# Three more places for expert weights, rows in chunk order and another order in the mix stage of a two-layer encoder step

## What is computed

```python
for i in range(2):
    proj = x @ w_in                       # split into attention, HGRN2 and gate columns
    a = latent_attention(...); o = hgrn2(...)
    merged = sigmoid(ga) * (a @ w_br_a) + sigmoid(gb) * (o @ w_br_b)
    x = layernorm(ALPHA * x + merged @ w_out, ln1_g, ln1_b)
    g_prob = softmax(x @ w_rg); e = softmax(x @ w_re within the top group); top 2 of 8
    moe = sum over the 2 experts of wts * ((silu(x @ w1[e]) * (x @ w3[e])) @ w2[e])   # 32 experts
    ple = sigmoid(x @ w_ple_gate) * (p[i] @ w_ple)
    x = layernorm(ALPHA * x + moe + ple, ln2_g, ln2_b)
```

## Time and profile before

| | us |
|---|---|
| median of 3 runs | 1827.39 |
| lowest, highest | 1825.66, 1830.17 |
| the profiled execution | 1829.14 |
| its span, first to last instruction | 1827.4 |

### The profile page before, as it was taken

How to read it: one execution, slowest core, us unless ns; L and a number is a source line. 1 busy time by engine, 2 the same in 40 slices (tenths; PEclk the granted TensorE clock), 3 DMA queues, 4 the chain that set the end, 5 groups by cost and what they waited for, 6 DMA issues and landing times.

```text
span 1827.4 us, 21052 instructions
## 1 busy us (share of the span) xinstructions
PE 1469.8 (80%) x8984; PEld 736.4 (40%) x8985; DVE 470.6 (26%) x1009; ACT 266.9 (15%) x649; POOL 49.7 (3%) x95
## 2 busy tenths in 40 slices
PE   5999879999977767766697998799999777577752
PEld 3556554554432223321253655545544332133310
DVE  3231661162110111100313417513512110111003
ACT  2332321111100000000134323111111000000001
POOL 1200000000000000000021000000000000000000
PEclk9999898998998889878798998799989997888886
DMA  8302213474999999999741032046469999999991
GB/s 296 114 1 93 98 52 128 170 291 167 426 426 426 426 427 426 426 427 426 288 166 48 2 134 102 11 164 244 176 250 426 426 426 427 426 426 427 426 427 79
DMA packets 97458, 491.04 MB, mean 269 GB/s; under 512 B 9264, under 2 KB 15184, under 8 KB 47696
## 3 DMA queue, kind: packets, MB, share of 16 engines
q1 hardware_dynamic: 92608, 478.16, 64.3%
q0 software_dynamic: 4752, 11.45, 1.9%
HBM read 486.69 MB, written 2.89 MB: 268 GB/s over the span
## 4 chain that ended last, share of the span: by engine, by line
PE 53%; DMA 22%; SPq 13%; DVE 5%; issue 3%; ACT 2%; DVEq 0%; POOL 0%; ACTq 0%
PE bank L785 50%; DMA ring<-in_w_e_up 14%; SPq L645 13%; DMA ring<-in_w_e_down 5%; DMA arena<-in_w_e_up 3%; PE bank L812 3%; DVE arena L1819 1%; DMA lnw<-in_ln_b 1%; DVE arena L1820 1%; DVE arena L1852 1%; PE bank L1217 0%; DVE arena L1644 0%; DVE x_sb L1644 0%; DVE x_sb L1649 0%; DVE x_sb L1651 0%
## 5 line engine op out<-in xcount | busy, mean ns | idle before, releaser
L785 PE MATMUL bank<-arena 128*32 128x512 f32 (+12 forms) x2392 | 596.4, 529 | 253.8 <-DMA ring<-in_w_e_up 82.3
L785 PE MATMUL bank<-ring,arena 128*32 128x512 f32 (+4 forms) x1976 | 489.8, 629 | 26.1 <-DMA arena<-in_w_e_gate 12.4
L785 PE MATMUL bank<-ring,xT 128*32 128x128 f32 (+5 forms) x2496 | 451.9, 398 | 7.9 <-issue 4.0
L785 PEld LDWEIGHTS bank<-arena 128*32 128x32 f32 (+7 forms) x2392 | 226.5, 154 | 574.3 <-issue 557.9
L785 PEld LDWEIGHTS bank<-ring,xT 128*32 128x32 f32 (+1 forms) x2496 | 221.9, 144 | 218.5 <-issue 198.9
L785 PEld LDWEIGHTS bank<-ring,arena 128*32 128x32 f32 (+1 forms) x1976 | 135.7, 132 | 122.6 <-issue 115.5
L785 PE MATMUL bank<-arena,x_sb 128*128 128x128 f32 (+1 forms) x768 | 146.0, 323 | 2.5 <-DVE arena L1982 1.9
L785 PE MATMUL bank<-cst,arena 128*32 128x512 f32 (+2 forms) x256 | 135.8, 672 | 0.1
L785 PEld LDWEIGHTS bank<-arena,x_sb 128*128 128x128 f32 (+1 forms) x768 | 111.5, 200 | 45.3 <-issue 16.9
L785 PE MATMUL bank<-lb,arena 128*32 128x512 f32 x160 | 88.4, 705 | 0.0
L2050 DVE TENSOR_TENSOR arena<-arena,bank 128x512 f32<-128x512 f32 x16 | 11.0, 688 | 275.1 <-PE bank L785 275.1
(11 more groups left out here) (218 smaller groups left out, 862.4 us busy)
## 6 DMA issues: line engine op xcount, KB each, us to landing
ring<-in_w_e_up SPq DMA_DIRECT2D x66, 1024.0 KB, 26.6
ring<-in_w_e_down SPq DMA_DIRECT2D x60, 1024.0 KB, 26.7
arena<-in_w_e_gate SPq DMA_DIRECT2D x58, 1024.0 KB, 25.7
ring<-in_w_e_gate SPq DMA_DIRECT2D x50, 1024.0 KB, 26.9
arena<-in_w_e_down SPq DMA_DIRECT2D x48, 1024.0 KB, 26.3
arena<-in_w_e_up SPq DMA_DIRECT2D x44, 1024.0 KB, 26.3
ring<-in_w_in SPq DMA_DIRECT2D x32, 1024.0 KB, 9.1
cst<-in_w_e_gate SPq DMA_DIRECT2D x10, 1024.0 KB, 26.5
```

Source lines behind the costliest of these rows:

```text
L785: return pe.matmul(out, lhsT, rhs, start=first, stop=last, skip_group_check=True)
```

## The change

- Slots: 9 arena slots in place of 7, and the place of the norm rows (LNW_SLOT) once per layer, for one piece of U of quad 0: 21 in place of 18. The working area before the slots shrinks by 768 words, since the input p (pin) now lies where the gathered tokens come later; the arena grows by 3328 words per partition, and the DMA scratch area shrinks to 4096 bytes.
- The host lays out x, the rows of LN0 and LN1 and those of LN2 of layer 0 in chunk order. x is loaded in place. In layer 0 the sums are kept in chunk order too (`by_chunks`), so that the banks are read with a stride of 8 when they are added; in layer 1, whose result is stored, all stays in the natural order.
- POOL loads LN2's rows after U of quad 0.
- Mix stage: the output product of tile 1's second half is cut in two (`project_half`) with the router of tile 0 between; the low product of tile 0 comes before the transposes of tile 1; the gate product of tile 0 is cut in two, around the ranks. DVE routes tile 0 before the last residual add.

```diff
-ARENA_SLOTS = 7
-LEVEL_SLOT, LB_SLOT, XT_SLOT = RING + ARENA_SLOTS, RING + ARENA_SLOTS + 1, RING + ARENA_SLOTS + 2
-SLOTS = RING + ARENA_SLOTS + 3
+ARENA_SLOTS = 9
+LEVEL_SLOT, LB_SLOT, XT_SLOT, LNW_SLOT = range(RING + ARENA_SLOTS, RING + ARENA_SLOTS + 4)
+SLOTS = RING + ARENA_SLOTS + 4
...
+def chunk_order(a):
+    return np.ascontiguousarray(a.reshape(a.shape[:-1] + (P, 8)).swapaxes(-1, -2).reshape(a.shape))
...
-            (("wo", 0, 1), 6), (("rt", 2), 7), (("t1", 0, 0), 0), (("t1", 0, 1), 1), (("wo", 1, 1), 2), (("rt", 0), 3),
-            (("pl", 0, 2), 4), (("pg", 0, 2), 5), (("t1", 1, 0), 6), (("t1", 1, 1), 7), (("pl", 0, 0), 0), (("rt", 1), 1),
-            (("pg", 0, 0), 2), (("rk", 0), 3), (("rk", 1), 6), (("rk", 2), 7), (("cnt",), 1),
+            (("wo", 0, 1), 6), (("rt", 2), 7), (("t1", 0, 0), 0), (("t1", 0, 1), 1), (("rt", 0), 3), (("wo", 1, 1), 2),
+            (("pl", 0, 2), 4), (("pg", 0, 2), 5), (("pl", 0, 0), 0), (("t1", 1, 0), 6), (("t1", 1, 1), 7), (("rt", 1), 1),
+            (("rk", 0), 3), (("rk", 1), 6), (("rk", 2), 7), (("cnt",), 1), (("pg", 0, 0), 2),
...
-    turns += [(2, i) for i in wo]
+    turns += [(2, i) for i in wo] + [(2.5, LNW_SLOT)]
...
-        turns.append((half, i))
+        if i != LNW_SLOT:
+            turns.append((half, i))
...
-        ARENA, FIRST_SLOT = 23520, 9184
+        FIRST_SLOT = 8416
+        ARENA = FIRST_SLOT + ARENA_SLOTS * SLOT
...
-        def sums(t, j):
-            return acc[:, t, 512 * j:512 * j + 512] if t < 2 else acc2[:, P * j:P * j + P]
+        def by_chunks(layer):
+            return layer < DEPTH - 1
+        def sums(layer, t, j):
+            if t == 2:
+                return acc2[:, P * j:P * j + P]
+            if by_chunks(layer):
+                return acc[:, t, :].rearrange("q (c p) -> q c p", c=8)[:, :, 64 * j:64 * j + 64]
+            return acc[:, t, 512 * j:512 * j + 512]
+        def for_sums(layer, t, b):
+            return by_chunk(b[:, :]) if t < 2 and by_chunks(layer) else b[:, 0:held(t)]
...
+                    elif i == LNW_SLOT:
+                        sp.wait_ge(ln_out, 3 * (2 * layer + 1) + 3)
...
-                sp.dma_start(x_given[0:NT[t], t, :], src).then_inc(x_in, 16)
+                sp.dma_start(x[0:NT[t], t, :], src).then_inc(x_in, 16)
...
                 load_ln(1 + 2 * layer, ln1_g[layer], ln1_b[layer])
+                job_done(pool, (layer, "moe", 0, "U"))
                 load_ln(2 + 2 * layer, ln2_g[layer], ln2_b[layer])
...
+            def project_half(layer, key, t, lhs, names, h):
+                n = piece_number(layer, names[h])
+                arrived(n)
+                b = open_bank((layer,) + key + (t,)) if h == 0 else bank((layer,) + key + (t,))
+                w = slot(n).rearrange("p (c n) -> p c n", c=4)
+                for c in range(4):
+                    ins = mm(b[0:NT[t], :], lhs[:, 4 * h + c, T0[t]:T0[t] + NT[t]], w[:, c, :], h + c == 0, h + c == 4)
+                if h == 1:
+                    done(ins)
...
                 turn_mixed(0)
-                mix(1, 1)
+                half_mix = lambda h: project_half(layer, ("wo", 1), 1, mT, [("wo", 1, 0), ("wo", 1, 1)], h)
+                half_mix(0)
                 router(0)
+                half_mix(1)
                 for t in range(3):
                     job_read(pe, (layer, "pT", t))
                 plain(0, 2)
+                plain_low(0, 0)
                 turn_mixed(1)
-                plain_low(0, 0)
                 router(1)
-                plain_high(0, 0)
+                half_gate = lambda h: project_half(layer, ("pg", 0), 0, xT, [("pg", 0, 0), ("pg", 0, 1)], h)
+                half_gate(0)
...
                 done(ins)
+                half_gate(1)
...
-                if k % 2:
-                    a, gain = x_chunks(t), by_chunk(gain)
-                else:
-                    a = src[0:n, :]
-                step(dve.scalar_tensor_tensor(a, a, mean, gain, ALU.subtract, ALU.mult))
+                step(dve.scalar_tensor_tensor(src[0:n, :], src[0:n, :], mvs[0:n, 2 * t:2 * t + 1], lnw[0:n, 0, :],
+                                              ALU.subtract, ALU.mult))
...
                 route_tile(2)
+                route_tile(0)
                 mixed(1, 1)
                 norm_mixed(1)
                 read_x("t1", layer, xT, (1,))
-                route_tile(0)
                 route_tile(1)
...
-                        emptied(dve.tensor_tensor(a, a, bank(key)[:, 0:a.shape[1]], ALU.add), key)
+                        emptied(dve.tensor_tensor(a, a, src, ALU.add), key)
...
-    nc = bacc.Bacc("TRN2", target_bir_lowering=False, num_devices=1)
+    nc = bacc.Bacc("TRN2", target_bir_lowering=False, num_devices=1, dynamic_dma_scratch_size=4096)
...
+    for n in ("x_prompt", "x_sample", "ln0_g", "ln0_b", "ln1_g", "ln1_b"):
+        arrays[f"in_{n}"] = chunk_order(arrays[f"in_{n}"])
+    for n in ("ln2_g", "ln2_b"):
+        rows = arrays[f"in_{n}"]
+        arrays[f"in_{n}"] = np.concatenate([chunk_order(rows[:-1]), rows[-1:]])
```

More of the change, by code:

```diff
@@ L303 @@
 SLOT_OF, FILLS, BEFORE = place_pieces()
+LNW_PIECES = [divmod(SLOT_OF[layer * LAYER_PIECES:].index(LNW_SLOT) - len(PIECES), len(MOE_PIECES)) for layer in range(DEPTH)]
+assert all(g == 0 and MOE_PIECES[i][0] == "eu" for g, i in LNW_PIECES)
 LEVELS_GONE = max(n for n in range(LAYER_PIECES) if SLOT_OF[n] == LEVEL_SLOT)
@@ L1551, in plain_gate @@
                     job_done(act, key)
-                    emptied(act.activation(sums(t, j), bank(key)[:, 0:held(t)], ACT.Sigmoid), key)
+                    emptied(act.activation(sums(layer, t, j), for_sums(layer, t, bank(key)), ACT.Sigmoid), key)
                 for t in MIX_ORDER:
@@ L2018, in gated @@
                 def gated(j, t):
-                    a, w = sums(t, j), held(t)
+                    a, w = sums(layer, t, j), held(t)
                     key = (layer, "pl", j, t)
@@ L2023, in gated @@
                     job_read(dve, (layer, "pg", j, t))
[L2024 removed]
+                    emptied(dve.tensor_tensor(a, a, for_sums(layer, t, bank(key)), ALU.mult), key)
                     if t < 2:
                         job_read(dve, key)
[L2027 removed]
+                        a = a if by_chunks(layer) else by_chunk(a)
+                        step(dve.scalar_tensor_tensor(a, x_chunks(t, w * j, w), ALPHA, a, ALU.mult, ALU.add))
                 def read_tokens(key):
@@ L2098, in more @@
                         for j in range(2):
-                            a = acc[:, t, 512 * j:512 * j + 512]
-                            dve.tensor_tensor(a, a, banks[2 * t + j][:, :], ALU.add)
+                            a = sums(layer, t, j)
+                            dve.tensor_tensor(a, a, for_sums(layer, t, banks[2 * t + j]), ALU.add)
                     a = acc2
@@ L2110, in _ @@
                 xt = acc_s[0:DEC, :]
-                step(dve.scalar_tensor_tensor(by_chunk(xt), x_chunks(2), ALPHA, by_chunk(xt), ALU.mult, ALU.add))
+                if by_chunks(layer):
+                    step(dve.scalar_tensor_tensor(xt, x[0:DEC, 2, :], ALPHA, xt, ALU.mult, ALU.add))
+                else:
+                    step(dve.scalar_tensor_tensor(by_chunk(xt), x_chunks(2), ALPHA, by_chunk(xt), ALU.mult, ALU.add))
                 layer_norm(2 + 2 * layer, 2, acc_s)
```

62 lines of the change are left out of this document (30 added, 32 removed).

## The result

| | before | changed kernel |
|---|---|---|
| median | 1827.54 us | 1800.80 us |
| lowest, highest | 1825.66, 1830.17 (4 runs) | 1799.12, 1801.73 (4 runs) |
| the profiled execution | 1829.14 us | 1801.73 us |
| its span | 1827.4 us | 1799.9 us |

The ratio is 0.985, with a 95% interval of 0.9835 to 0.9864: 26.7 us less. The forecast was 1801. That it came so near was partly luck: the two large terms, the streams and the gather, came as forecast, but four others were off (the norm at the start, the norm at the end of layer 0, the order of the mix stage, the scratch area), and their errors cancelled. The views of the changed kernel show which.

The account below looks back on a forecast made before the run. DMA was taken to bound each layer's expert stream, PE and its waits the rest. Slots 9.0, norms 1.6, mix order 2.2 and gather clock 14.6 sum to 27.4 us less: 1801 us, range 1797 to 1806.

Parts of the forecast that it names:

- Slots: Expert streams: three more pieces placed before each stream save 7.4 us, LN2's rows cost 2.9; net 4.5 per layer, 9.0 in all.
- the third slot: Piece at the norm rows' place, before each stream: saves 2.5 us, but LN2's rows then cost 2.9, so about nothing.
- The clock in the gather: First gather before quad 0: dense half product ahead keeps full clock, 8.5 us; gain 7.3 per layer, 14.6 in all.
- Rivals 1 and 2: Clock still falls in the first gather: in one layer, 1808 us, chance 0.14; in both, 1816 us, chance 0.09.
- Order of the mix stage: Output product of tile 1 to gather: reordering takes 25.9 us, gaining 3.2 and 1.6; net 2.2 after a clock allowance.
- The term for the fall: Mix stage: waits of about 0.9 and 0.8 us around the transposes may lower the clock; 1.3 us per layer, between 0 and 3.
- Norms at the start: Tile 0 of LN0: contiguous scale-and-shift takes 1.285 us instead of 2.07, 0.79 less on the path.
- Norm at the end of layer 0: Tile 0 of LN2: contiguous scale-and-shift is 0.79 us shorter on the path; 1.6 together with the start.
- Sums in chunk order: Layer 0 adds reading the bank at a stride of 8 cost nothing: 0.69 us against 0.689 contiguous.
- Scratch: DMA scratch of a quarter: costs between 0 and 1 us, taken as 0, judged by POOL's mask loads.
- Rivals 3 and 4: PE frees slots too late, streams get gaps: 1810 us, chance 0.04; or the stream's rate falls: 1842 at 405 GB/s, 0.04.

Follow-up runs that it names:

- no_lnw: Changed kernel with 9 arena slots but no piece at the place of the norm rows, and LN2's rows loaded early again: 1798.96 us.
- gate_split_only: Kernel before with one edit, the gate product of tile 0 cut in two around the ranks: 1813.71 us, ratio 0.9928.
- gate_whole: Changed kernel with the gate product of tile 0 in one piece before the ranks: 1811.01 us.
- order_undone: Changed kernel with the old order of the mix stage: 1810.81 us.
- fill: Changed kernel with tile 0's gate product cut in eight steps, placed before tile 1's transposes, before its router, and around the ranks: 1791.38 us, ratio 0.9797.
- scratch_only: Kernel before with the DMA scratch cut to 4096 bytes and nothing else: 1823.46 us, ratio 0.9978.
- best: fill with ACT taking the reciprocal root of tile 0 in LN2 before it copies the sample's sums: 1792.33 us.
- slots_undone: Changed kernel with 7 arena slots, no piece at the place of the norm rows, and LN2's rows loaded early again: 1804.76 us.
- rows_late: no_lnw with LN2's rows loaded after U of quad 0, as in the changed kernel: 1803.38 us.
- order_only: Kernel before with the new order of the mix stage alone; slots, rows and sums as before: 1817.07 us, ratio 0.9952.

## Why the prediction came out right, and where it didn't

**Slots: right.** 9.0 was forecast, 9.4 is there by the stage table, 9.8 by the windows that answer to the earlier trace rows. The price of the LN2 rows, 2.9 from the shares of three windows, measured 3.4, and one piece 3.2 where 2.47 was forecast. If these two are misses at all, they cancel in the net. That the third slot is worth nothing was told and is shown by no_lnw.

**The clock in the gather: right**, in size (7.4 for 7.3 per layer) and in its condition (dense work just ahead). It's the largest term, and gate_split_only gives it alone. The earlier trace rows had the price, 8.48, and the earlier trace rows the state that it replaced. Rivals 1 and 2 did not come about in any of the 18 profiled gathers with a dense product directly before them. What they said of the gather has to be put otherwise, though: it isn't a fall just ahead that is kept, for the kernel before enters its gather at 2.4 GHz and loses it 2 us later, and the prediction's "it stayed down for all of it" was read from a window that begins 3 us in the earlier trace rows. The fall follows what came before it, at a distance that differs between kernels with the same instructions there: 2 us into the gather in the kernel before, behind its end in layer 0 of gate_whole.

**Order of the mix stage: wrong.** The waits forecast, 0.9 and 0.8, are 0.82 and 0.83, but the gain is not that of the new order. The sum came to 25.9 from the output product to the gather and credited the new order with the 3.2 and 1.6 us that this is below. order_undone has 25.85 in both layers with the old order: the contiguous norms are enough. What the new order adds is the second wait and the fall of the clock behind it. The term for the fall, 1.3 us per layer, measured 1.9 in layer 0 (27.77 less the 25.9 of the sum) and 3.5 in layer 1 (29.42 less 25.9); the bound given, 3, was exceeded. The 3.26 for 1.88 of the earlier trace rows was read as the size of such a fall. It was only as long as what stood there: a product of 1.88 us. This time a router and a half product stood under the fall, 1.3 + 2.1 us more in layer 1. A net gain of 2.2 was forecast for the two layers, and there was a loss of 0.6. fill shows the price from the other side: with the waits closed, 3.2 and 4.9 us come back, 1.65 of each the waits themselves.

**Norms at the start: the 0.8 did not arrive.** The scale-and-shift is at 1.28 us, as forecast, and the first transposes start 0.7 us earlier (15.93 for 16.60). But behind them PE now waits for its weights. The first two rows of the changed kernel's PE timeline:

```profile
15.93 1.94 PE L849 MATMUL bank<-cst,x_sb 128*128 128x128 f32 x8 [15.93 <-DVE x_sb L1686]
18.97 7.86 PE L811 MATMUL bank<-ring,xT 128*128 128x384 f32 x16 [1.10 <-DMA ring<-in_w_in]
```

The product is 0.3 earlier (19.26 before, then behind ACT's copy) and takes 7.86 for 7.31; the third tile's starts at 34.88 for 34.62. Its length is no effect of the change: the same product takes 7.03 in fill and 8.04 in scratch_only. The step that failed is that the sum never asked what comes next behind the norm: it was the transfer of w_in, in every kernel here with the contiguous norm. The remaining -0.9 before 388.63 isn't explained by a row of this stage, and equal kernels differ by as much there (scratch_only).

**Norm at the end of layer 0: 0.1 instead of 0.8.** Two things stood in the way. The smaller is an instruction that the change made slower and that the sum had left out. ACT moves the sample's sums in four copies, now read with a stride of 8 and written in runs of 16: 1.65 us became 2.63. The reciprocal root of tile 0 stands behind them. ACT's and DVE's timelines of the changed kernel:

```profile
885.79 2.63 ACT L1661 COPY arena<-arena 32x256 f32<-32x256 f32 x4 [4.88 <-DVEq L2144]
...
888.77 0.20 ACT L1348 ACTIVATE small<-small 128x1 f32<-128x1 f32 x1
```

```profile
889.09 1.29 DVE L1686 SCALAR_TENSOR_TENSOR x_sb<-arena,small,lnw 128x1024 f32<-128x1024 f32 x1 [0.32 <-ACT small L1348]
```

0.32 of wait is new, so the norm of tile 0 ends 4.53 us after LN2's first statistics where it was 5.02. But PE's transposes begin at 5.70 for 5.83 (891.54 and 904.29), and in best, where the norm ends at 4.25, at 5.65. The views name no releaser for PE there in these two kernels ("issue"); they leave out what its sequencer does by itself. The trace has that instruction, the COMPARE_BRANCH of line 576 (567 in the kernel before), which skips the further passes over crowded experts. Times in us from LN2's first statistics:

```
                  branch lasts   it ends   the norm ends   first transpose
before                6.01         5.67        5.02             5.83
changed               5.87         5.53        4.53             5.70
best                  5.80         5.49        4.25             5.65
gate_split_only       5.19         4.86        5.03             5.09
slots_undone          4.59         4.27        4.54             4.59
```

The first transpose follows whichever ends last: in 12 of the 14 profiles it starts 0.16 or 0.17 behind the branch, in the two others, where the branch is over before the norm, 0.05 or 0.06 behind the norm. So the step that failed is the path. In the kernel before the norm was already done 0.65 us before the branch, and a faster norm had next to nothing to give. Why the same branch takes between 4.6 and 6.1 us the runs don't show. The stage up to the output product of layer 1 did gain 0.8, but only 0.1 of it here, and among the profiles it varies by more than that.

**Sums in chunk order: free, as the row said.** The adds of layers 0 (stride 8) and 1 (contiguous) stand in one row, the answer to the earlier trace rows, and the largest is 690 ns for both:

```profile
L2105 DVE TENSOR_TENSOR arena<-arena,bank x80: 420/689/690, 477.9 to 1778.1; 128x512 f32<-128x512 f32 x64, 128x256 f32<-128x256 f32 x16
```

The Trainium skill ("SBUF — State Buffer", "Door 1: The DMA port swizzle") says that PSUM has 8-byte lines and that a non-contiguous pattern there slows matmuls; these adds are reads by VectorE, and they show no slowdown. The norm's reads and writes in SBUF with the same stride did cost 0.79 us for 1024 columns, and all of them are gone:

```profile
L1683 DVE SCALAR_TENSOR_TENSOR x_sb<-x_sb,small,lnw x9: 1271/1285/1285, 13.2 to 1292.1; 128x1024 f32<-128x1024 f32 x6, 32x1024 f32<-32x1024 f32 x3
```

**Scratch: wrong.** It was bounded at 0 to 1 us of cost, from POOL's issues of masks, and those are unchanged. The gain of 3.9 us was outside the bounds, since only the middle of the program was looked at, not its end. The prediction had nothing for the tail ("Layer 1 ends with the old order: nothing"); no row of it was read, though 24 us of the profile lie there.

The sum was right to a microsecond by luck: the scratch's 3.9 and small gains of the streams and the gather (0.6) stood against 1.7 at the start and 2.8 in the two mix stages. Rivals 3 and 4 have nothing for them either: the streams have no gap and no lower rate. Without the scratch the time would have been about 1804.7 (1800.8 + 3.9), still inside the 1797 to 1806 of the forecast.

## What to carry to other kernels

Before a long run of small or medium matmuls, put a dense piece that is due anyway directly ahead of it, and use the rest of it to close waits of under a microsecond: here cutting one gate product around the ranks gave 14 us, and cutting it finer took 8.6 off the changed kernel. A move whose gain comes together with another edit should be run without that edit: the new places in the mix stage looked like a gain and were a loss. Price a fall of the clock by the work that follows it, not by the row in which it was last seen. When memory is shuffled to win buffers, look for what else the freed area or the new layout touches (the copies on ACT, the drain at the end), and ask of each shortened step what is late next, the engine's own branches included.

## What the runs showed of the hardware

- GpSimd's DRAIN at the end of the program lasts 6.84, 3.25 and 2.92 us with a DMA scratch area of the default size, 8192 and 4096 bytes.
- A gather of 48 matmuls of 128 columns takes 8.41 us at 2.4 GHz, and all 18 first gathers with a dense product directly before them kept that clock. Where the clock falls at its first matmul it takes 14.97 (order_undone, layer 1), and the clock doesn't come back within it; it comes back in G, the product of 512 columns behind it.
- A wait of 0.82 us, transposes and a wait of 0.83 us are followed by a fall of the clock in layer 0 of all six profiles that have them, within 2 us behind the second wait. In layer 1 the same instructions and waits are followed by one in both profiles of the changed kernel and in rows_late, but in none of slots_undone, no_lnw and gate_whole at that place. order_only, with 2.38 in place of 0.82, has one in both layers. What decides isn't in these rows.
- 1 MiB of broadcast rows on POOL's queue costs the weight stream 3.4 us; 1 MiB of weights less shortens it by 2.5 (by the rate) to 3.2 (at LNW). Equal kernels differ by up to 2 us in this stage.
- PE's sequencer spends 4.6 to 6.1 us in one COMPARE_BRANCH over a skipped part at the end of layer 0, in all 14 profiles, and in 12 of them it is what PE's next product starts behind.
